# Natural panels as half the contraction by 512 columns, with four token tiles open and the sums of squares of the heads on VectorE

## The reference, cut to what matters

```python
h = rmsnorm(x, g_mix); z = h @ w_in
u, va, q, k, v, gate_a, gate_b = split(z)        # 512, 512, 3 x 1536, 2 x 1024 columns
u = gelu(u); va = rmsnorm(gelu(va), g_v)
a = chunk_mix(u, va, w_s, b_s)
q = rotary(rmsnorm(q, g_q)); k = rotary(rmsnorm(k, g_k))      # per head of 64
b = dilated_attention(q, k, v, caches)           # 3 groups of 8 heads, 129 keys
x += (sigmoid(gate_a) * (a @ w_oa) + sigmoid(gate_b) * (b @ w_ob)) @ w_o
x += relu(rmsnorm(x) @ w_ff1) ** 2 @ w_ff2
x += sigmoid(rmsnorm(x) @ w_ple_gate) * (p @ w_ple_proj)
```

## Time and profile before

| | |
|---|---|
| median of 3 runs | 1040.69 us |
| the profiled execution's span | 1041.0 us |
| natural stage | 14 to 350 us |
| busy over the whole span: PE, DVE, ACT, POOL | 98%, 74%, 50%, 24% |
| instructions PE, DVE, ACT, POOL | 8310, 1004, 1253, 381 |

### The profile page before, as it was taken

The page is one execution under the profiler, slowest core; times in us unless marked ns, Lnnn a source line. Parts: engine busy times, 40 slices in busy tenths (PEclk is TensorE's granted clock), DMA queues, the critical chain, the costliest instruction groups (busy, mean ns, idle before and its releaser), DMA issues.

```text
span 1041.0 us, 20872 instructions
## 1 busy us (share of the span) xinstructions
PE 1023.5 (98%) x8310; PEld 1008.5 (97%) x8310; DVE 774.4 (74%) x1004; ACT 518.5 (50%) x1253; POOL 245.6 (24%) x381
## 2 busy tenths in 40 slices
PE   9999999999999999999999999999999999999997
PEld 7999999999999999999999989999999999999997
DVE  6679888988899878999674368747856875786553
ACT  6773797658845574352264385414522531453332
POOL 2441233122312003958201211100100100012300
PEclk9999999999999999999999999999999999999999
DMA  6557556776687765776843335655664574573412
GB/s 186 192 178 231 200 177 208 227 242 206 208 256 213 210 218 148 224 218 186 258 142 122 122 122 208 214 183 172 229 209 152 195 247 168 171 252 130 162 54 86
DMA packets 131634, 195.89 MB, mean 188 GB/s; under 512 B 32321, under 2 KB 109473, under 8 KB 129746
## 3 DMA queue, kind: packets, MB, share of 16 engines
q1 hardware_dynamic: 107616, 125.51, 37.9%
q0 software_dynamic: 10560, 63.28, 18.3%
q10 hardware_dynamic: 13362, 5.77, 2.0%
HBM read 185.55 MB, written 62.00 MB: 238 GB/s over the span
## 4 chain that ended last, share of the span: by engine, by line
PE 66%; DVE 13%; ACT 5%; issue 5%; DMA 5%; POOL 3%; SPq 3%; ACTq 0%; DVEq 0%; POOLq 0%
PE gm L1347 26%; PE gm L1603 7%; PE psSO L1603 4%; PE gm L1321 4%; PE gm L1322 3%; PE gm L1323 3%; PE psT L1603 3%; DMA w_raw<-in_w_in 3%; PE psSO L1651 2%; PE psSO L1347 2%; PE psT L1347 2%; PE psT L1651 2%; DVE w_lo L1708 2%; POOL kv L2363 2%; ACT prob L1123 2%
## 5 line engine op out<-in xcount | busy, mean ns | idle before, releaser
L1321 PE MATMUL gm<-w_hi,h_hi 128*128 128x256 f32 x640 | 186.9, 292 | 1.1 <-DVE w_lo L1708 0.9
L1322 PE MATMUL gm<-w_hi,h_lo 128*128 128x256 f32 x640 | 180.8, 282 | 0.0
L1323 PE MATMUL gm<-w_lo,h_hi 128*128 128x256 f32 x640 | 180.1, 281 | 0.0
L1347 PE MATMUL gm<-h_hi,w_hi 128*128 128x272 f32 x624 | 132.7, 294 | 0.4 <-ACT z L852 0.4
L1347 PE MATMUL gm<-h_hi,w_lo 128*128 128x272 f32 x624 | 130.0, 290 | 0.0
L1347 PE MATMUL gm<-h_lo,w_hi 128*128 128x272 f32 x624 | 129.4, 289 | 0.0
L1321 PEld LDWEIGHTS gm<-w_hi,h_hi 128*128 128x128 f32 x640 | 120.8, 189 | 3.1 <-issue 1.7
L1323 PEld LDWEIGHTS gm<-w_lo,h_hi 128*128 128x128 f32 x640 | 121.2, 189 | 0.0
L1322 PEld LDWEIGHTS gm<-w_hi,h_lo 128*128 128x128 f32 x640 | 120.6, 188 | 0.0
L2352 POOL DMA_DIRECT2D out_kvs<-in_cache_kv_w x64 | 35.0, 547 | 345.2 <-PE gm L1347 120.6
L1708 DVE TENSOR_TENSOR w_lo<-w_raw,w_hi 128x1024 fp32r<-128x1024 f32 x76 | 90.5, 1228 | 21.3 <-ACT w_hi L755 20.8
(11 more groups left out here) (378 smaller groups left out, 2662.7 us busy)
## 6 DMA issues: line engine op xcount, KB each, us to landing
out_kvs<-in_cache_kv_w POOLq DMA_DIRECT2D x64, 510.0 KB, 4.7
w_raw<-in_w_in SPq DMA_DIRECT2D x60, 512.0 KB, 6.2
w_raw<-in_w_ff SPq DMA_DIRECT2D x36, 512.0 KB, 5.7
kv<-in_cache_kv_w SPq DMA_DIRECT2D x128, 128.0 KB
kv<-in_cache_kv_w SPq DMA_DIRECT2D x64, 256.0 KB
out_kvs<-in_cache_kv_w POOLq DMA_DIRECT2D x32, 508.0 KB, 5.3
w_more<-in_w_ff SPq DMA_DIRECT2D x26, 512.0 KB, 6.1
kv<-in_cache_kv_w POOLq DMA_DIRECT2D x128, 64.0 KB, 3.3
```

Source lines behind the costliest of these rows:

```text
L1321: nc.tensor.matmul(out, lh, wh, start=k == 0, stop=False)
L1322: nc.tensor.matmul(out, ll, wh, start=False, stop=False)
L1323: last = nc.tensor.matmul(out, lh, wl, start=False, stop=k == KD - 1)
L1347: last = nc.tensor.matmul(pair[:, half, 0:HALF], w, x[:, k0 + k, half * HALF:(half + 1) * HALF], start=first, stop=end)
```

## The change

A natural panel becomes half of the contraction (512 rows) by 512 columns. Two panels make one kind of one group, a **section**, in five PE slots; I call them A (tiles 0 and 1, first half of the contraction), B (tiles 2 and 3, first half), S (samples, whole contraction), C (tiles 0 and 1, second half) and D (tiles 2 and 3, second half). A tile slot has 24 matmuls of 512 columns instead of 48 of 256, S has 16 of 512. There are ten sections, so 50 slots instead of 60 units. Each of the four banks of `gm` holds one tile from A or B until C or D. The outputs of a section (samples, tiles 0, 1, 2, 3) are taken by ACT and DVE one per slot, two slots late (`OUT_OF`), so that tile 2 is taken in slot A of the next section and tile 3 in slot B. PE waits for the copy of tile `a` before it starts tile `a` of the next section.

The banks of `gm` are no longer there for scores: `psS` and `psO` take them, both pieces of a pair always together, and the values go through the transposes' banks. The samples use `psO` too, so one mask comes after their join. Sums of squares: ACT makes one `Square` of 128x512 (L876), DVE sums it by heads (`sum_heads`, L1870). `fin` has a buffer for each parity of the tile; a tile's rotation waits for the transposes of the tile two before, and for k of groups 1 and 2 also for the store of it, which now goes tile by tile. The two halves of the split fall in slots A and C (`late_split`); on DVE they come behind the scores' maximum and the first chunk. Six of the chunks that stood in the natural stage move behind it (60 before, 54 after).

```diff
-COLS = {"oa": 512, "ob": 512, "pj": 1024}
+COLS = {"oa": 512, "ob": 512, "pj": 1024, "q": 512, "k": 512, "v": 512, "va": 512}
+TILES = (SAMPLES, 0, 1, 2, 3)
+OUT_OF = {_s: [_s - 2] if 2 <= _s < N0 else [N0 - 2, N0 - 1, N0] if _s == N0 else [_s] if _s > N0 else [] for _s in range(U_FF)}
 def summed_by_act(u):
-    return UNITS[u][1] in ("k", "q")
+    return False
 def late_split(s):
-    _, kind, _, _, sub = UNITS[s]
-    return sub == 0 and (kind in NATURAL or kind == "oa")
+    _, kind, _, _, sub = SLOT[s]
+    return sub in (0, 3) if s < N0 else sub == 0 and kind == "oa"
+PAIR_SLOT = [14, 18, 19, 23, 24, 28, 29, 33, 34, 38, 39, 43, 44, 48, 50, 52]
+CHUNKS_IN_SLOT = ("00000" "00012" "11213" "22111" "02101" "11213" "22111" "02101" "11213" "21101"
...
 def s_bank(j):
-    return gm[:, 3] if score_bank(j) else psS[:]
+    return (psS, psO)[score_bank(j)][:]
...
+                    nc.scalar.copy(z[:, r, 0:512], src).then_inc(unit_out, 1)
+                    if kind != "va":
+                        act.wait_ge(unit_out, u + 1)
...
+                            nc.scalar.activation(sq[:, r, 0:512], z[:, r, 0:512], ACT.Square, scale=HD ** -0.5).then_inc(sq_ready, 1)
...
+            def natural_tiles(s):
+                p, x = SLOT[s][0], s % 5
+                half, first = x // 3, 5 * (s // 5)
+                for n in range(2):
+                    a = 2 * (x % 3) + n
+                    out, tile = gm[:, a], slice(128 * a, 128 * a + 128)
+                    if half == 0 and first:
+                        pe.wait_ge(unit_out, first - 5 + TILES.index(a) + 1)
...
+                    for kk in range(4):
+                        k = 4 * half + kk
+                        if n == 0 and x == 0:
+                            panel_split(p, 512, kk)
...
+                        nc.tensor.matmul(out, h_hi[:, k, tile], wh, start=k == 0, stop=False, skip_group_check=True)
...
+                if prev is not None:
+                    if tile != SAMPLES:
                         dve.wait_ge(t_ready, TINDEX[("qk", prev)] + 1)
-                    if fin_count(n - 3):
-                        dve.wait_ge(fin_stored[n % 3], fin_count(n - 3))
+                    if fin_count(prev):
+                        dve.wait_ge(fin_stored[head_buffer(u)], fin_count(prev))
...
+            def sum_heads(u):
+                rows, r, n = shape_kq(u), (zc(u) - 1) % 2, kqn(u)
+                a, c = root_place(n)
+                dve.wait_ge(sq_ready, sq_count(u))
+                vec.tensor_reduce(st[heads_rows(u), a, c:c + H], sq[0:rows, r, 0:512].rearrange("p (h d) -> p h d", d=HD), AX.X,
+                                  ALU.add).then_inc(ssq_ready, 1)
```

More of the change, by code:

```diff
@@ L240 @@
 SLOTS = U_FF
-COPY_AT = [s for s in range(0, 96, 3) if s not in (48, 51, 54, 57)] + [97, 99, 100, 102]
-V_BACK = {35: (1, 0), 39: (1, 1), 53: (2, 0), 57: (2, 1)}
-X_STEPS = {10: (2,), 13: (3,), 14: (4,)}
+COPY_AT = list(range(0, 81, 3)) + [82, 87, 89, 90, 92]
+V_BACK = {34: 1, 48: 2}
+X_STEPS = {5: (2,), 6: (3, 4)}
 TJOBS = {}
@@ L297, in _plan_sjobs @@
     for s in range(SLOTS):
-        jobs = []
-        if s in S_AT and not (paired(S_AT[s]) and S_AT[s] % 2):
-            jobs.append(("piece", S_AT[s]))
-            if paired(S_AT[s]):
-                jobs.append(("piece", S_AT[s] + 1))
-        for job in jobs:
+        for job in [("piece", j) for j in PAIR_AT.get(s, [])]:
             SJOBS.setdefault(s, []).append(job)
@@ L312, in small_steps @@
 def small_steps(s):
-    t, sc = TJOBS.get(s, []), [x for x in SJOBS.get(s, []) if not (paired(x[1]) and x[1] % 2)]
-    steps = [("transposes", x) for x in t if x[0] == "qk"] + [("scores", x) for x in sc if x[0] == "piece"]
-    steps += [("transposes", x) for x in t if x[0] != "qk"] + [("scores", x) for x in sc if x[0] != "piece"]
-    if s - 2 in S_AT:
-        steps.append(("values", S_AT[s - 2]))
-    return steps
+    t, sc = TJOBS.get(s, []), SJOBS.get(s, [])[:1]
+    steps = [("transposes", x) for x in t if x[0] == "qk"] + [("scores", x) for x in sc]
+    return steps + [("values" if x[0] == "pv" else "transposes", x) for x in t if x[0] != "qk"]
 STEPS = {s: small_steps(s) for s in range(SLOTS)}
@@ L563, in wait_values @@
         def wait_values(engine, g):
[L565 to L566 removed]
+            engine.wait_ge(v_stored[g], V_STORES[g])
         FIN_STORES = [0, 0, 0]
@@ L1277, in small_step @@
                 else:
-                    values(what)
+                    values(what[1])
             def between(u, g, groups):
@@ L1292, in between @@
                     n_steps = len(STEPS[u - 1])
+                    if u < N0 and u % 5 == 1:
+                        groups = 4
                     for n in range(n_steps):
@@ new lines, in natural_samples @@
+            def natural_samples(s):
+                p, first = SLOT[s][0], 5 * (s // 5)
+                if first:
+                    pe.wait_ge(unit_out, first - 5 + 1)
+                else:
+                    pe.wait_ge(h_lo_done, KD + 1)
+                if LAST_EXP_BEFORE[s]:
+                    pe.wait_ge(exp_done, LAST_EXP_BEFORE[s])
+                for k in range(KD):
+                    if k >= 4:
+                        panel_split(p, 512, k - 4)
+                    both, cols = hs[k // 4][:, k % 4], slice(k % 4 * 512, k % 4 * 512 + 512)
+                    nc.tensor.matmul(psO[0:2 * NS], both, w_hi[:, k // 4, cols], start=k == 0, stop=False)
+                    last = nc.tensor.matmul(psO[0:2 * NS], both, w_lo[:, k // 4, cols], start=False, stop=k == KD - 1)
+                    if k < KD - 1:
+                        between(s, k, KD)
```

598 lines of the change are left out of this document (293 added, 305 removed).

## The result

The changed kernel takes 1115.34 us, median of four runs (1111.09 to 1118.94); the kernel before, beside it, 1043.08 (1040.42 to 1045.89). The ratio is 1.0686, interval 1.064 to 1.0733: slower, by some 72 us, and above the forecast's range, which ended at 1104. The sign was right, the size half: +36 forecast.

A forecast was written before the change was run, and what follows sets the result against it. The prediction took PE, busy 98% of the span, as the bound. Parts 1 to 7 summed to +29.9 us and the clock added 6, so 1041.0 became 1077 us, with a range of 1046 to 1104.

The forecast's parts named there:

- Part 8: PE's clock falls to half behind a third of about thirteen new waits, four falls: +6 us (0 to 20).
- Part 1: Natural-stage matmuls: 960 of 512 columns at 0.2258 us replace 1920 of 256, sample matmuls halve: -13.7 us.
- Part 7: End of the natural stage: `u` waits for ACT, +5 us (2 to 9); chunks moved behind it, +3 (0 to 12).
- Part 2: Squares and sums: ACT loses 82.6 us, DVE gets 16.6 us of sums; ACT's relief is worth nothing by itself.
- Part 3: Slot A: PE waits for ACT's copy to free tile 2's bank, +16.6 us (ends 10 and 22).
- Part 4: Section starts: PE waits for DVE's `w_lo` split behind maxima, scale and chunk, +9 us (4 to 13).
- Part 5: Sections 2 and 3: DVE's load of 68 us exceeds PE's 57.4, so DVE falls behind, +4 us (0 to 8).
- Part 6: k of groups 1 and 2: rotation of tiles 2 and 3 waits for earlier tiles' stores, +6 us (0 to 14).
- Rival (c): The clock falls after every wait and stores land in 7 us or more: 1097 us (1092 to 1112), chance 0.13.

The follow-up runs named there:

- x4: The changed kernel with the squares and sums of q and k back on ACT: 1117.64 us, ratio 1.0701 to the kernel before.
- y4: y3 with another table of sample chunks, fewer in sections 2 and 3 and one fewer behind the stage: 1080.68 us, ratio 1.0378.
- z1: y3 with a table of 57 chunks in the natural stage instead of 54, two less in sections 2 and 3: 1082.38 us, ratio 1.0362.
- x1: The changed kernel with unread matmuls on PE ahead of the natural stage's waits for `w_lo` and tile 2's bank: 1105.02 us, ratio 1.0582.
- x6: x1 with unread matmuls also at the start of `u`, ahead of `V` and ahead of the samples' maximum: 1100.27 us, ratio 1.0535.
- z2: z1 with ACT's cast of the next panel behind the copy of `qT` and `kT` in slots that begin a section: 1069.57 us, ratio 1.0251.
- x2: The changed kernel with tile 2's copy and square ahead of the pair's exponentials and mask on ACT: 1113.04 us, ratio 1.0641.
- x3: The changed kernel with the `w_lo` split ahead of the scores' maxima, scale and chunk on DVE: 1117.43 us, ratio 1.0705.
- y1: The changed kernel with tiles 2 and 3 both copied on ACT ahead of that slot's copies of probabilities: 1109.67 us, ratio 1.0675.
- y3: y1 plus the split right behind the maxima, the last four pairs' values a slot later and some ACT work earlier at the stage's end: 1096.22 us.

## Why the prediction was half right

The mechanism was foreseen: PE waits where the small pieces had covered ACT and DVE. What failed is above all Part 8, the clock, then the gain of Part 1; among the waits, the samples' maximum behind Part 7's chunks was not named and cost more than the 3 us that stood for them, and the reload of `V` had no term.

**Part 1, mis-sized.** The timeline of PE in after, ten starts apart:

```profile
58.95 0.39 PE L1347 MATMUL gm<-w_hi,h_hi 128*128 128x512 f32 x1
...
61.27 0.39 PE L1348 MATMUL gm<-w_hi,h_lo 128*128 128x512 f32 x1
```

(61.27 - 58.95)/10 = 0.232 us a matmul, where 0.2258 was taken. The gain on two of 256 is 960 x (0.239 - 0.232) = 6.7 us, and the samples lost some 0.6 instead of gaining 1.0: some 6 us where 13.7 were forecast. The step that failed is the constant remainder: 512 columns at 2.4 GHz are 0.2133, so 0.0187 is left over, not 0.0125. The Trainium skill, "TensorE: Matmul & The Clock Gate", section "Back-to-back issue gap", gives 0.216 by its formula for the isolated gap; the trace has 0.232, and the measurement decides.

**Part 2, right** (x4). The 24 sums in after's natural stage, group of DVE (busy, mean ns, idle before), took 16.5 us, with 16.6 forecast:

```profile
L1870 DVE TENSOR_REDUCE st<-sq 128x8 f32<-128x512 f32 x24 | 16.5, 686 | 0.8
...
L1854 DVE TENSOR_TENSOR fin<-z,gk_b 128x512 f32<-128x512 f32 x12 | 8.3, 689 | 20.6 <-DMA out_kvp<-fin 20.4
```

**Part 3, right.** Forecast 1.0, three times 2.4 and three times 2.8: 16.6. Measured 0.69, then 2.33, 2.03, 2.03, then 2.64, 2.64, 2.63: 15.0. The chain on ACT in after is the one derived from the earlier trace rows; it begins with the second transposition's copy at 147.63 and ends at 151.28 (the last row is PE's):

```profile
147.63 0.59 ACT L983 COPY PT<-psT 128x512 f32<-128x512 f32 x1 [1.25 <-PE psT L1482]
...
148.44 0.83 ACT L1153 ACTIVATE prob<-psSO,O_blk 128x256 f32<-128x256 f32 x2
149.30 0.59 ACT L1047 CAST psSO<-masks 128x512 f32<-128x512 bf16 x1
...
150.69 0.59 ACT L870 COPY z<-gm 128x512 f32<-128x512 f32 x1
151.33 0.50 PE L1347 MATMUL gm<-w_hi,h_hi 128*128 128x512 f32 x1 [2.33 <-ACT z L870]
```

**Parts 4 and 5, right in sum.** At the sections' starts, behind q: 5.03 and 2.85 us; behind k: 2.35 and 1.16; behind v: 1.53 and 0.31. That is 13.2, for 9 + 4. (Part 5's five tiles add up to 14.7 us, not 15.6, which moves nothing.) Two earlier waits for `w_lo`, 1.44 at 72.58 and 1.57 at 88.28, were not foreseen. The longest has the order that was drawn, two maxima, the scale and a chunk ahead of the split on DVE, while PE stands for 5 us (the first and the last row are PE's, the others DVE's):

```profile
130.19 1.16 PE L1544 MATMUL psSO<-kT,qT 64*128 64x128 f32 x16
...
134.65 1.28 DVE L1930 TENSOR_REDUCE O_blk<-psSO 128x2 f32<-128x512 f32 x2
135.96 0.69 DVE L1878 TENSOR_TENSOR vn<-vn,st 32x512 f32<-32x512 f32 x1
...
138.00 2.35 DVE L1744 TENSOR_TENSOR w_lo<-w_raw,w_hi 128x1024 fp32r<-128x1024 f32 x2
139.36 0.76 PE L1347 MATMUL gm<-w_hi,h_hi 128*128 128x512 f32 x1 [5.03 <-DVE w_lo L1744]
```

But the scores were there at 131.35, and DVE took their maximum only 3.3 us later: most of the 5 us is DVE's backlog, Part 5, and less of it Part 4's chain, whose chunk took 1.4 here and not 2.45. y4 and z1, where this wait is gone with fewer chunks in sections 2 and 3, bear that out.

**Part 6, too high.** The rotation of k did wait for the store, 20.4 us in all (the row of L1854 above), once 7.0 us at 196.5. But behind that PE waited for nothing until 222.25 us; whether the 1.53 us there hang on the store isn't shown. No run took the store's wait away.

**Part 7, half.** `u` waited 3.90 and 2.32 us for ACT, 6.2 for 5. The chunks moved behind the stage were taken at 3; PE waits 8.4 us at one place. At 547.15 PE waits for the samples' maximum, in front of which DVE's list still has chunks (DVE in after, each chunk a product and a reduction):

```profile
541.64 1.22 DVE L1942 TENSOR_TENSOR kv<-kv,Qb 128x1024 f32<-128x1024 f32 x1
542.89 1.22 DVE L1943 TENSOR_REDUCE sc<-kv 128x16 f32<-128x1024 f32 x1
...
546.70 0.30 DVE L1961 TENSOR_TENSOR sc<-sc,sm 128x136 f32<-128x136 f32 x1
```

The prediction said that the slots ahead of this place have slack and PE needs DVE only for splits; PE also needs this maximum, and z1, with a chunk less ahead of it, waits 3.9 us. The reload of `V`, 4.7 us, was not in the prediction at all. Its four DMAs stand on SP behind others, and issuing them takes long (SP's queue in after):

```profile
370.48 2.55 SPq L675 DMA_DIRECT2D kv<-in_cache_kv_w  x4
373.08 10.41 SPq L723 DMA_DIRECT2D V<-out_kvp  x4
```

**Part 8 failed: the clock.** All waits together were forecast at 16.6 + 9 + 4 + 6 + 5 + 3 = 43.6 us and measured at 50.7: 7 too low. The clock was forecast at 6 and at most 20; the account has 24 while PE worked. "About thirteen" waits over 1.5 us became seventeen, and of the eighteen of 1.4 or more eleven, not a third, had the clock fall. The falls lasted 61.47/11 = 5.6 us on average, six of them 3.4 as the one before, the others 6.8 or 10.2; the prediction took 3. So both factors, how often and how long, came from a single fall, and both were too low. Rival (c), where the clock falls behind every wait, was the nearest case, at 1097; it too took the length of a fall from that one row. Misses of 7 (waits), 18 (clock) and 8 (matmuls) are 33 of the 34 us between the forecast and the span.

That the clock follows PE's idling is shown by x1 and x6. The Trainium skill, "TensorE: Matmul & The Clock Gate", section "Why this matters for your kernels", warns of idle gaps between bursts of matmuls from a certain length on. The traces agree that idling brings the lower clock, with 0.94 in 140 to 366 us where PE idles and 1.00 where matmuls fill the waits; but waits of 2.03 us, shorter than the gaps that the page means, had a fall too, and there the measurement decides.

That 45 us are a matter of order (where each instruction and each chunk stands) is shown by z2. What of the rest could still go isn't shown: z2's waits for `w_lo` and for `u` were not tried further.

## What to carry to other kernels

A kernel whose bound engine has hardly a wait pays for fewer, larger pieces with the waits that the small ones covered; list for each piece what the other engines' lists hold between its last input and its release. On TensorE price each new wait together with the half-clock work that may follow it: here 50.7 us of idling cost another 24 us of clock, 16 of which came back with the clock kept up. And when a wait is taken away by moving one instruction ahead, look at what it passes: x2, x3 and y1 alone won nothing that is clear of the noise, and the gain came when what they had made late was moved too (y3, z2) and the chunks were dealt out anew (y4, z1).

## What the runs showed of the hardware that was not expected

- Waits of 2.03 us had a fall of the clock (at 191.33 and 232.04), while one of 2.64 at 274.31 and one of 2.33 at 151.33 had none. The two at 191.33 and 232.04, and that of 2.64 at 314.54, each came some 10 us behind another wait (2.35, 1.53 and 1.16 us); but so did the two without, 12 us behind 2.85 and 5.03 us. The runs don't settle which wait brings a fall.
- 512 columns start 0.232 us apart at the higher level and 0.427 at the lower: (391.53 - 390.25)/3. At the higher level 0.0187 is left over, at the lower nothing.
- Issuing the four DMAs that reload `V` took SP 10.41 us, 2.6 each, where four loads of `kv` took 2.55 together.
